# Hybrid decoder step on one core: deeper rings of weight halves, gathers interleaved, low halves moved between engines

## The reference, cut to what matters

```python
q = (xb @ w_q).reshape(PEER_BLOCK, PEER_HEADS, 2, D_KEY // 2)
s = jnp.einsum('thpc,pnc->thpn', q, sub_keys)
sv, si = lax.top_k(s, PEER_TOPK)
cand = sv[:, :, 0, :, None] + sv[:, :, 1, None, :]
best, flat = lax.top_k(cand.reshape(...), PEER_TOPK)
idx = i1 * N_KEYS + i2                    # 8 heads x 16 of 16384 experts per row
gate = jax.nn.softmax(best, axis=-1)
act = jax.nn.gelu(jnp.einsum('thkd,td->thk', u_tab[idx], xb))
out = jnp.einsum('thk,thkd->td', (gate * act), v_tab[idx])
```

## Time and profile before

| what | us |
|---|---|
| median of 3 runs | 1557.59 |
| the profiled execution, its own time | 1566.55 |
| its span in the trace | 1564.7 |
| TensorE matmuls busy | 1372.6 (88%) |
| VectorE busy | 1000.1 (64%) |
| ScalarE busy | 667.7 (43%) |
| GpSimd busy | 359.3 (23%) |
| queries / ungated / gated / V, stage lengths | 80 / 253 / 282 / 445 |
| one high half on ScalarE; one Gelu pair (L1642, L1645) | 0.63; 0.37 + 0.22 |
| load of a half, median from issue to landing: u; v | 2.7; 3.1 |

### The profile page before, as it was taken

The page is one execution under the profiler, slowest core; times in us unless marked ns, Lnnn a source line. Parts: engine busy times, 40 slices in busy tenths (PEclk is TensorE's granted clock), DMA queues, the critical chain, the costliest instruction groups (busy, mean ns, idle before and its releaser), DMA issues.

```text
span 1564.7 us, 24623 instructions
## 1 busy us (share of the span) xinstructions
PE 1372.6 (88%) x8950; PEld 1177.7 (75%) x8950; DVE 1000.1 (64%) x1850; ACT 667.7 (43%) x1492; POOL 359.3 (23%) x284
## 2 busy tenths in 40 slices
PE   6999865998796998899999999999999159799997
PEld 5987632787434988889999999999877147677775
DVE  4556788444523248999327777777677147677776
ACT  4432042231002454344456666666555125455554
POOL 1110131001100015475661000000334743222210
PEclk9999676999888999999999999999999679999998
DMA  6430200000132334444546444444577158888864
GB/s 219 136 120 28 115 16 1 1 1 28 31 161 91 121 100 130 133 139 145 167 140 195 125 126 127 129 126 125 163 257 255 41 195 263 276 272 278 277 217 135
DMA packets 117612, 219.26 MB, mean 140 GB/s; under 512 B 31649, under 2 KB 32161, under 8 KB 116513
## 3 DMA queue, kind: packets, MB, share of 16 engines
q1 hardware_dynamic: 106272, 184.78, 37.5%
q0 software_dynamic: 11264, 33.60, 6.5%
HBM read 207.64 MB, written 10.42 MB: 139 GB/s over the span
## 4 chain that ended last, share of the span: by engine, by line
PE 41%; DVE 10%; POOL 7%; DMA 4%; issue 4%; ACT 3%; SPq 0%; ACTq 0%; DVEq 0%; POOLq 0%
PE ph L1702 9%; PE ph L1703 8%; PE ph L1704 8%; PE acc L1772 4%; POOL RT L1590 4%; PE pg L1753 4%; PE acc L1774 4%; PE acc L1773 4%; DVE ohx L1934 3%; POOL lo L1579 2%; ACT hi L1612 2%; DMA raw<-in_v 2%; DVE lo L1787 1%; DVE hid L1812 1%; DVE hid L1809 1%
## 5 line engine op out<-in xcount | busy, mean ns | idle before, releaser
L1612 ACT ACTIVATE hi<-raw 128x512 fp32r<-128x512 f32 x544 | 341.6, 632 | 483.0 <-PE acc L1774 203.2
L1787 DVE TENSOR_TENSOR lo<-raw,hi 128x512 fp32r<-128x512 f32 x448 | 313.7, 709 | 209.8 <-ACT hi L1612 208.2
L1702 PE MATMUL ph<-xh,hi 128*128 128x320 f32 x1152 | 366.4, 318 | 27.4 <-DVE lo L1787 20.8
L1703 PE MATMUL ph<-xl,hi 128*128 128x320 f32 x1152 | 358.1, 311 | 0.0
L1704 PE MATMUL ph<-xh,lo 128*128 128x320 f32 x1152 | 357.9, 311 | 0.0
L1772 PE MATMUL acc<-hi,ch 128*128 128x512 f32 x512 | 207.6, 405 | 74.8 <-DVE cl L1945 74.7
L1702 PEld LDWEIGHTS ph<-xh,hi 128*128 128x128 f32 x1152 | 218.5, 190 | 33.7 <-DVE lo L1787 22.9
L1703 PEld LDWEIGHTS ph<-xl,hi 128*128 128x128 f32 x1152 | 218.6, 190 | 0.0
L1704 PEld LDWEIGHTS ph<-xh,lo 128*128 128x128 f32 x1152 | 218.1, 189 | 0.0
L1774 PE MATMUL acc<-lo,ch 128*128 128x512 f32 x512 | 201.9, 394 | 0.0
L1773 PE MATMUL acc<-hi,cl 128*128 128x512 f32 x512 | 201.7, 394 | 0.0
(11 more groups left out here) (360 smaller groups left out, 1890.9 us busy)
## 6 DMA issues: line engine op xcount, KB each, us to landing
raw<-in_uT SPq DMA_DIRECT2D x256, 256.0 KB, 2.7
raw<-in_v SPq DMA_DIRECT2D x256, 256.0 KB, 3.1
wraw<-in_w_in SPq DMA_DIRECT2D x30, 512.0 KB, 3.5
raw<-in_w_q SPq DMA_DIRECT2D x32, 256.0 KB, 2.8
wo<-in_w_out SPq DMA_DIRECT2D x4, 1024.0 KB, 10.7
h_scratch<-act_s SPq DMA_DIRECT2D x128, 32.0 KB, 2.5
sth<-in_state_h SPq DMA_DIRECT2D x1, 2048.0 KB, 7.6
out_hgrn_s<-stn SPq DMA_DIRECT2D x1, 2048.0 KB, 6.9
```

What stands on the lines that cost most here:

```text
L1612: act.activation(wide(hi[n % 4]), wide(raw[n % 4]), ACT.Copy).then_inc(t_hi, 1)
L1702: pe.matmul(o, hi[s][:, k], xh[:, c], start=begin, stop=False)
L1703: pe.matmul(o, hi[s][:, k], xl[:, c], start=False, stop=False)
L1787: dve.tensor_tensor(wide(lo[n % 4]), wide(raw[n % 4]), wide(hi[n % 4]), ALU.subtract).then_inc(lo_v, 1)
```

## The change: what it does, and the diff

The rings of `hi` and `lo` get eight places (halves n and n - 8 share one). `raw` keeps four places until half UM = UV + 80 (V block 40), then gets eight, the four new ones in places of `hid` that V has used up; so do the four buffers of fetched rows (`vbuf`, now in `hid` blocks 0 to 15). ScalarE runs three blocks ahead of TensorE in making `hi` (two blocks ahead in V), and does its Gelu pair before the next high halves and not after them. The spills move from SP's queue to ScalarE's. GpSimd makes all 128 low halves of the ungated stage and `share()` goes. GpSimd issues the first 16 cells as soon as all spills have landed, waits for V block 15, and then issues two cells behind each row fetch until all 64 are out; VectorE waits for cells in four groups of 16. Pick k runs in V block 20 + 13k/8. TensorE's loop bodies hold four blocks instead of two, the transposes come after block 55. The final adds of the picked rows come in V blocks 123 and 126 instead of 120 and 125, and SP copies `upper` behind all loads. Cut to its core:

```diff
-        NPICK, EARLY = 64, 16
+        NPICK = 64
         WQ = 2 * NQ
-        EXP_AT, PICKED = NA // 2 - 4, NA // 2 - 3
-        ACC_AT = {10 + 5 * k // 3: k for k in range(NPICK)}
+        RAW, RING = 4, 8
+        EXP_AT, PICKED = NA // 2 - 4, NA // 4 - 2
+        CHUNK = 16
+        ACC_AT = {20 + 13 * k // 8: k for k in range(NPICK)}
...
-        hi = [big_mem.sb(f"hi{u}", [P, 4, P], F32R) for u in range(4)]
-        lo = [big_mem.sb(f"lo{u}", [P, 4, P], F32R) for u in range(4)]
+        hi = [big_mem.sb(f"hi{u}", [P, 4, P], F32R) for u in range(RING)]
+        lo = [big_mem.sb(f"lo{u}", [P, 4, P], F32R) for u in range(RING)]
...
-        vbuf = [big_mem.sb(f"vbuf{r}", [P, D]) for r in range(4)]
+        vbuf = [hflat[:, D * r:D * r + D] for r in range(4)]
...
-        hs_out = [sem(f"hs_out{r}") for r in range(4)]
+        hs_out, hs_past = [*x_in, sh_in], 16
...
-        hsel_in = [sem(f"hsel_in{r}") for r in range(2)]
+        hsel_in = [sem(f"hsel_in{c}") for c in range(NPICK // CHUNK)]
...
+        MORE = 32
+        UM = UV + 2 * MORE + 16
+        raw_in = [*t_in, *w_in_slot]
+        raws = [wide(r) for r in raw] + [hflat[:, 4 * D + 4 * P * r:4 * D + 4 * P * r + 4 * P] for r in range(4)]
+        assert 4 * D + 16 * P <= MORE * DT and UM % 8 == 0
+
+        def raw_at(n):
+
+            if n < UM:
+                return raws[n % RAW], t_in[n % RAW], 16 * (n // RAW + 1)
+            past = 16 * (UM // RAW) if n % 8 < RAW else wo_in[n % 8 - RAW]
+            return raws[n % 8], raw_in[n % 8], past + 16 * ((n - UM) // 8 + 1)
+
+        def raw_freed(n):
+
+            return n - RAW if n < UM else max(n - 8, UM - 4 + n % 8 % RAW if n < UM + 4 else 0)
...
-                    if n >= 4:
-                        sp.wait_ge(*lo_of(n - 4))
+                    if n >= RAW:
+                        sp.wait_ge(*lo_of(raw_freed(n)))
+                    if n == UM + RAW:
+                        sp.wait_ge(c_lo, MORE)
...
                 for n in range(UE):
...
-                    b = (n - UA - 9) // 2
-                    if n % 2 and 0 <= b < NBLK:
-                        sp.wait_ge(hs_done, b + 1)
-                        sp.dma_start(hs_dram[b], act_s[b % 4][:]).then_inc(hs_out[b % 4], 16)
                     if n == UV + NBLK + 3:
                         sp.wait_ge(c_lo, NBLK // 2)
                         sp.dma_start(x2, x1_dram[0:DT].rearrange("(i p) d -> p i d", i=2)).then_inc(rows_in, 16)
                         sp.dma_start(nf, inp["norm_f"].to_broadcast([P, D])).then_inc(rows_in, 16)
                         sp.dma_start(xs, x1_dram[DT:NT]).then_inc(rows_in, 16)
-                    if n == UE - 10:
-                        sp.wait_ge(v_used, NPICK + 1)
-                        sp.dma_start(upper[0:ST], va[0][ST:2 * ST]).then_inc(rows_in, 16)
+                sp.wait_ge(v_used, NPICK + 1)
+                sp.dma_start(upper[0:ST], va[0][ST:2 * ST]).then_inc(rows_in, 16)
...
-                    if n == UA + 4 * (PICKED + 1):
+                    if n == UA + 8 * PICKED + 4:
                         pool.wait_ge(rt_ready, 2)
                         pool.memset(hflat[:, DIRTY:MID], 1.0).then_inc(ones_set, 1)
-                    if n % 4 != 3:
-                        pool.wait_ge(t_hi, n + 1)
-                        pool.tensor_tensor(wide(lo[n % 4]), wide(raw[n % 4]), wide(hi[n % 4]), ALU.subtract).then_inc(lo_p, 1)
+                    pool.wait_ge(t_hi, n + 1)
+                    pool.tensor_tensor(wide(lo[n % RING]), wide(raw[n % 4]), wide(hi[n % RING]), ALU.subtract).then_inc(lo_p, 1)
...
-                def cells(c, first, end):
+                pool.wait_ge(id_ready, 1)
+                for r in range(4):
+                    pool.wait_ge(hs_out[r], hs_past + 16 * (NBLK // 4))
+                def cells(first, end):
                     for k in range(first, end):
                         pool.indirect_dma_start(out=hsel[:, k:k + 1], out_offset=None, in_=hs_cells,
                                                 in_offset=bass.IndirectOffsetOnAxis(ap=cell_id[:, k:k + 1], axis=0)) \
-                            .then_inc(hsel_in[c], 16)
-                pool.wait_ge(id_ready, 1)
-                pool.wait_ge(rt_ready, 2)
-                for k in range(4):
+                            .then_inc(hsel_in[k // CHUNK], 16)
+                cells(0, CHUNK)
+                pool.wait_ge(c_lo, 4 * D // DT)
+                for k in range(NPICK):
                     rows(k)
-                for r in range(4):
-                    pool.wait_ge(hs_out[r], 16 * (NBLK // 4))
-                cells(0, 0, EARLY)
-                for k in range(4, EARLY):
-                    rows(k)
-                cells(1, EARLY, NPICK)
-                for k in range(EARLY, NPICK):
-                    rows(k)
+                    cells(min(CHUNK + 2 * k, NPICK), min(CHUNK + 2 * k + 2, NPICK))
...
                 def high(n):
-                    act.wait_ge(t_in[n % 4], 16 * (n // 4 + 1))
-                    if n >= 4:
-                        act.wait_ge(t_mm, n - 3)
-                    act.activation(wide(hi[n % 4]), wide(raw[n % 4]), ACT.Copy).then_inc(t_hi, 1)
+                    source, landed, count = raw_at(n)
+                    act.wait_ge(landed, count)
+                    if n >= RING:
+                        act.wait_ge(t_mm, n - RING + 1)
+                    act.activation(wide(hi[n % RING]), source, ACT.Copy).then_inc(t_hi, 1)
...
+                for n in range(6):
+                    high(n)
                 for m in range(NQ + 1):
                     if m < NQ:
-                        high(2 * m)
-                        high(2 * m + 1)
+                        high(2 * m + 6)
+                        high(2 * m + 7)
                     if m >= 1:
...
 
-                high(UA)
-                high(UA + 1)
+                def spill(b):
+                    act.wait_ge(hs_done, b + 1)
+                    act.dma_start(hs_dram[b], act_s[b % 4][:]).then_inc(hs_out[b % 4], 16)
+
...
+                    if b:
+                        hidden(b - 1)
+                    if b == 2 * EXP_AT - 4:
                         act.wait_ge(e_in, 3)
                         act.activation(best_flat, best_flat, ACT.Exp).then_inc(e_out, 1)
+                    high(UA + 2 * b + 6)
+                    high(UA + 2 * b + 7)
+                    if b:
+                        spill(b - 1)
                     if NA - 4 <= b < NA:
                         if b == NA - 4:
...
-                    if b:
-                        hidden(b - 1)
...
-                    if v < NBLK - 1:
-                        high(UV + 2 * v + 2)
-                        if v == 0:
-                            hidden(NBLK - 1)
-                        high(UV + 2 * v + 3)
+                    if v == 1:
+                        hidden(NBLK - 1)
+                        spill(NBLK - 1)
+                    if 1 <= v < NBLK - 2:
+                        high(UV + 2 * v + 4)
...
-                    for u in range(4):
-                        if u % 2 == 0 and not first:
-                            pe.wait_ge(hs_done, 2 * i + (u // 2 - 1))
-                        if u < 3:
-                            pe.wait_ge(lo_p, 3 * i + (u + 1))
-                        else:
-                            pe.wait_ge(lo_v, i + (WQ + 1))
-                        unit(ph[:, u // 2, 0:NT], u, u % 2)
+                    for u in range(RING):
+                        if u % 2 == 0 and (u >= 4 or not first):
+                            pe.wait_ge(hs_done, 4 * i + (u // 2 - 1))
+                        pe.wait_ge(lo_p, 8 * i + (u + 1))
+                        unit(ph[:, u // 2 % 2, 0:NT], u, u % 2)
...
-                    for c in range(2):
-                        if not first:
-                            pe.wait_ge(g_used, 2 * i + (c - 1))
-                        pe.wait_ge(oh_ready, 2 * i + (c + 1))
+                    for c in range(4):
+                        if c >= 2 or not first:
+                            pe.wait_ge(g_used, 4 * i + (c - 1))
...
-                with pe.Fori(1, NG // 2) as i:
+                with pe.Fori(1, NG // 4) as i:
...
-                with pe.Fori(1, NBLK // 2 - 1) as i:
+                with pe.Fori(1, NBLK // 4 - 1) as i:
...
-                    dve.tensor_tensor(wide(lo[n % 4]), wide(raw[n % 4]), wide(hi[n % 4]), ALU.subtract).then_inc(lo_v, 1)
-                shared = [0]
-
-                def share():
-
-                    low(UA + 4 * shared[0] + 3)
-                    shared[0] += 1
...
+                for n in range(UB, UB + 4):
+                    low(n)
                 for g in range(NG):
                     one_hots(g)
-                    low(UB + 2 * g)
+                    low(UB + 2 * g + 4)
                     if g >= 1:
                         times_gates(g - 1)
-                    low(UB + 2 * g + 1)
+                    low(UB + 2 * g + 5)
                     if g >= 2:
```

(32 more changed lines are left out.)

76 lines of the change are left out of this document (30 added, 46 removed).

## The result

The changed kernel takes **1457.89 us** (median of 4 runs, 1449.14 to 1466.44) against 1557.44 for the kernel before in the same comparison: ratio **0.9359, 95% interval 0.9294 to 0.9424**. It is faster by 6.4%, and the forecast of 1455 was 3 us low. The execution that was profiled took 1466.44 us (span 1464.6); the sum of the prediction, for such an execution, was 1463.5.

A forecast was written before the change was run, and what follows sets the result against it. TensorE was taken as the gated stage's bound, with gains left in V and the ungated stage. Terms +0.9 - 2.8 - 21.4 - 79.7 = -103.0 took the median 1557.6 to 1454.6, forecast 1455 us, range 1438 to 1492.

The forecast's parts named there:

- Start of queries: Before the first query copy: ScalarE makes eight halves with four raw places, TensorE waits; +0.9 us (0 to +4).
- Ungated: Ungated stage: TensorE's waits for low halves go, leaving transposes, fill and gated entry; 229.7 against 251.1 us, -21.4.
- Rival B: Ungated stage: GpSimd becomes the bound, needing 220 us, and two stretches no longer recover; +12 to +22 us, chance 0.12.
- GpSimd beside VectorE: Ungated stage: GpSimd makes 128 low halves in 195 of 225 us; the skill's exclusion rule would give 205.
- Gated: Gated stage: no change, 282 us, as deeper rings buy nothing where nobody waits.
- Rival C: Loops: four-block bodies may outgrow the instruction store, each pass waiting for code; 1617 us, or 1495 if only gated; chance 0.08.
- V, cells: V, pick 16: cells 16 to 31 arrive long before it, so VectorE's wait goes; -49.5 us.
- V, picks: V, at picks: earlier halves remove TensorE's waits for `cl` and slow restarts; -27 us, with 6 kept for gaps.
- rival A: V: VectorE stays late at picks, nine tenths busy and in order; +21 us, 1476, chance 0.18.
- V, the 6 us of gaps: V: 6 us kept for gaps that stay; nothing charged for DMA at 310 GB/s, as the deeper ring hides late loads.
- V, big loads: V near block 65: three loads still delay the next half, SP standing four blocks; 10.5 us instead of 9, +1.5.
- Rival D: V: SP's wait at block 63 empties the ring, 16 us and a second dip; 1462, counted within the forecast's 0.62.

The follow-up runs named there:

- fill_last: Changed kernel with GpSimd's fill of ones moved behind all low halves of the ungated stage: 1458.54 us, ratio 0.9337 to the kernel before.
- gated_body_of_16: Changed kernel with TensorE's gated loop at 16 blocks a body and 3 passes, not 4 and 15: 1459.71 us, ratio 0.9349 to the kernel before.
- short_lead: Changed kernel with V's lead in making high and low halves put back to that of the kernel before: 1484.91 us, ratio 0.9520 to the kernel before.
- raw_places_early: Changed kernel with eight raw places from V block 16, picks from block 28 every 1.5 blocks: 1452.59 us, ratio 0.9320 to the kernel before.
- raw_four_to_end: Changed kernel with the raw places kept at four to the end: 1474.76 us, ratio 0.9458 to the kernel before.
- ungated_lead_four: Changed kernel with ScalarE's high halves in the ungated stage at most four ahead of TensorE, not eight: 1551.41 us, ratio 0.9938 to the kernel before.

## Why the prediction was right, step by step

- **Start of queries** (+0.9, four raw places for eight halves): TensorE waits 0.99 us there. Right. **Start of ungated** (-2.8): no gap. Right.
- **Ungated** (229.7): measured 230.6 from 577.3 to 807.9. The sum is right by two errors: the entry to the gated stage cost 0.9 and not 2.5, with a spill's issue on ScalarE that costs nothing (below), the lower end of what the prediction allowed; and the fill of ones behind `rt_ready` cost 2.8 (fill_last) and not 1.0: while GpSimd, now the maker of all lows, stands in it, no raw place comes free. GpSimd held: 0.4 us of waits for it. Rival B falls.
- **GpSimd beside VectorE**: GpSimd's 128 low halves took 186.7 us, where the rows had given 195. The estimate by the Trainium skill's rule (SBUF — State Buffer, SBUF: two separate sides) had been 205. Here the rows were nearer, and the stage stayed TensorE's, as by either.
- **Gated** (282): 282.2. No loop return costs anything. Rival C falls, but not by the sign that the prediction gave: the 11 packets of the earlier trace rows are in a queue that TensorE's longer program leaves as it is; TensorE's code shows in the other, with none before, two now and eight with sixteen blocks in the body (gated_body_of_16). The loop before makes 31 passes, not 29. The Trainium skill (Runtime: NRT & Kernel Launch, Instruction fetch mechanics) has a taken branch whose target lies outside the current two pages wait for a fetch; no stretch here shows such a stall, with four blocks or sixteen in the body. The same section of the Trainium skill gives TensorE's instruction store as 2048 instructions, more than the 1,024 matmuls and weight loads that the trace shows for sixteen blocks.
- **V, cells** (-49.5): alone they give -44.7, the wait and clock as predicted less 5 us, most of it new waits for `cl`. With the deeper rings those are gone too.
- **V, picks** (-27, with 6 kept for gaps): taking the lead back costs 25.2 us. Right in size and cause; rival A falls. The argument also leaned on "picks come never in three blocks running"; that holds for the kernel before as well, and in short_lead it goes with 46 waits.
- **V, the 6 us of gaps and "I charge nothing; the deeper ring hides late ones"**: this step failed in its reason. A load of a half takes 4.5 (places in `raw`) or 5.2 us (in `hid`) from issue to landing in V, for 3.1 before, and the ring of raw places is deep only from block 40. Before that four places wait beside the row fetches: waits of 0.6 to 2.0 us in blocks 24 to 42, and 4 to 7 us of V in all, which raw_places_early wins. The 6 us kept for gaps paid for it by chance.
- **V, big loads** (10.5): they cost 7.5 to 8.8 for SP's standing and 1.9 for the burst, some 10 us, with 12.0 as the whole difference of V. The size is right; the split was not. I put 1.5 us on SP's standing and 9 on the burst; with eight places it is the other way round. With four the burst is dear without long standing (raw_four_to_end, and the kernel before: 6.5 us). Rival D's mechanism is the one that acts, at less than its price.
- **Tail**: 8.7 us, unchanged.

In sum V took 365.8 us for the predicted 364.7, and the kernel 1466.4 for 1463.5.

## What to carry to other kernels

A ring is as deep as its shallowest part: eight products over four sources still wait for the sources, and the place to look is the stretch in which the sources are few. A wait that an engine or queue meets before it is due stops everything queued behind it: SP's wait for block 63 cost some 8 us and its 1.8 MB two, and ScalarE's early wait in ungated_lead_four cost 90; put such a step where its condition already holds. When two executions of one program differ, compare the start of each stage first: here the difference lay ahead of anything that was changed.

## What the runs showed of the hardware that was not expected

The granted clock of one and the same code is not the same in each execution: 0.66 to 1.00 in the window from 150 to 160 us over fourteen profiles, and 0.68 to 0.78 from 140 to 225. The longer stretch is the one to read: two executions with 0.66 in the short window start their queries at 488.9 and at 501.8. In all the first query matmul starts between 488.9 and 502.9 us, about as much as a kernel's times differ on one chip (1550.84 to 1568.74 us for the kernel before in the last comparison).

Here a transfer issued from ScalarE costs it nothing beside its own work. In the ungated stage of the changed kernel, with an issue, and in V, without (two activations in one row):

```profile
701.79 0.63 ACT L1623 ACTIVATE hi<-raw 128x512 fp32r<-128x512 f32 x1
701.93 0.33 ACTq L1662 DMA_DIRECT2D h_scratch<-act_s  x1
702.31 0.63 ACT L1623 ACTIVATE hi<-raw 128x512 fp32r<-128x512 f32 x1
...
1266.11 1.14 ACT L1623 ACTIVATE hi<-raw 128x512 fp32r<-128x512 f32 x2
```

The pair takes 1.15 us with an issue of 0.33 us inside it, and 1.14 without. In the 33 pairs of this kind from 580 to 770 us it takes 1.15 or 1.16 us each time.
